# A two-layer diffusion block on one core: modulation vectors summed in 32-column groups of TensorE, and scan scores taken from 64-row halves

## The reference, cut to what matters

```python
def modulate(x, shift, scale):
    return rms(x) * (1.0 + scale) + shift

for layer in range(2):                                  # layer 0: scan mixers, layer 1: attention
    m_l = split(silu(c)     @ w_mod[layer] + b_mod[layer], 6)    # w_mod[layer]: 1024 x 6144
    m_c = split(silu(c_ctx) @ w_mod[layer] + b_mod[layer], 6)
    z = concat([modulate(xc, m_c[0], m_c[1]), modulate(xl, m_l[0], m_l[1])])
    if layer == 0:
        p = z @ even_w_in
        ya = rwkv7_mix(p[:A_PROJ])                      # a scan with a 64x64 state per head, 8 heads, 2 directions
        yb = rglru_mix(p[A_PROJ:])                      # a gated diagonal scan, 512 wide, 2 directions
        y = concat([ya, yb]) @ even_w_out
    else:
        y = diff_attention(z)
    x = x + m[2] * y
    x = x + m[5] * peer_ffn(modulate(x, m[3], m[4]))    # 8 heads x 16 experts per token, gathered from tables

def rwkv7_step(state, r, w, k, v, kk, akk):             # for each token, head and direction
    sa = state @ kk
    state = state * w - outer(sa, akk) + outer(v, k)
    return state, state @ r
```

## Time and profile before

| what | value |
|---|---|
| median of three runs | 3483.07 us (3481.43 to 3484.12) |
| the profiled execution | 3485.71 us, of which the span of the trace is 3483.9 us |
| busy share of the span | PE 80%, DVE 65%, POOL 31%, ACT 20% |
| `modulation` | 9.6 to 90.8 us |
| `project_even` | 111.6 to 333.8 us |
| `rglru` | 333.8 to 391.6 us |
| `rwkv_scan` | 391.6 to 957.5 us |
| the rest of layer 0 and all of layer 1 | 957.5 us to the end |
| DMA rate in the expert stages | 420 GB/s in most slices of the page |

### The profile page before, as it was taken

The page is one execution under the profiler, slowest core; times in us unless marked ns, Lnnn a source line. Parts: engine busy times, 40 slices in busy tenths (PEclk is TensorE's granted clock), DMA queues, the critical chain, the costliest instruction groups (busy, mean ns, idle before and its releaser), DMA issues. The chain is left out here.

```text
span 3483.9 us, 31043 instructions
## 1 busy us (share of the span) xinstructions
PE 2802.4 (80%) x8972; PEld 1425.2 (41%) x8972; DVE 2254.0 (65%) x5072; ACT 701.0 (20%) x1707; POOL 1090.5 (31%) x941
## 2 busy tenths in 40 slices
PE   7697399999967999777787878787696578887777
PEld 1242288888834444322232223232344344432222
DVE  7697423332343767788887888888244367787887
ACT  2112433233102111111111111111104111111111
POOL 0010232122011444444444444444000034444443
PEclk9798699899878999999999999999899899999999
DMA  8552000000014999999999999999300189999998
GB/s 315 185 195 90 33 1 1 1 1 1 1 73 180 362 378 371 413 420 420 420 413 420 421 420 413 418 420 410 148 24 3 74 347 420 420 415 420 421 420 342
DMA packets 133878, 927.54 MB, mean 266 GB/s; under 512 B 16764, under 2 KB 17788, under 8 KB 31380
## 3 DMA queue, kind: packets, MB, share of 16 engines
q0 software_dynamic: 113472, 830.62, 58.1%
q1 hardware_dynamic: 20312, 95.72, 7.4%
HBM read 925.13 MB, written 1.15 MB: 266 GB/s over the span
## 5 line engine op out<-in xcount | busy, mean ns | idle before, releaser
L1370 PE MATMUL psum<-ring,diag 128*128 128x512 f32 x3072 | 1483.8, 622 | 374.7 <-DVE diag L1459 372.7
L1267 POOL DMA_INDIRECT ring<-in_uv,experts x768 | 914.4, 1191 | 1375.4 <-PE psum L1370 1017.9
L1481 DVE CUSTOM_DVE_ANT_0 ring<-ring,hcur 128x1024 f32<-128x1024 f32 x768 | 941.5, 1226 | 261.0 <-DMA ring<-in_uv,experts 240.2
L1370 PEld LDWEIGHTS psum<-ring,diag 128*128 128x128 f32 x3072 | 557.4, 194 | 1276.5 <-DVE diag L1459 799.4
L1301 ACT ACTIVATE gel<-dots 128x1 f32<-128x1 f32 x768 | 143.6, 201 | 1325.4 <-DVE dots L1481 1324.8
L1459 DVE TENSOR_SCALAR diag<-ident,gel,wcur 128x128 f32<-128x128 f32 x768 | 256.8, 345 | 80.2 <-ACT gel L1301 78.0
L385 PE MATMUL psum<-zT,wring 128*128 128x512 f32 x368 | 164.3, 604 | 15.7 <-DMA wring<-in_w_in 15.7
L1015 DVE COPY_PREDICATED T<-level,psum 128x512 f32<-128x512 uint32 x80 | 58.7, 734 | 180.6 <-PE psum L820 180.6
L1350 PE MATMUL psum<-hT,w_q 128*128 128x512 f32 (+3 forms) x512 | 163.1, 473 | 1.4 <-DMA w_q<-in_w_q 1.4
L1543 PE MATMUL psum<-wring,zT 128*128 128x512 f32 x320 | 140.1, 601 | 10.2 <-DMA wring<-in_w_qkv 10.2
L444 DVE SCALAR_TENSOR_TENSOR acc<-wmod,scol,acc 128x512 f32<-128x512 f32 x168 | 126.3, 752 | 6.9 <-ACT acc L411 1.2
(11 more groups left out here) (314 smaller groups left out, 2903.9 us busy)
## 6 DMA issues: line engine op xcount, KB each, us to landing
wring<-in_w_mod SPq DMA_DIRECT2D x12, 2048.0 KB, 9.7
wmod<-in_w_mod POOLq DMA_DIRECT2D x12, 2048.0 KB, 8.4
w_q<-in_w_q SPq DMA_DIRECT2D x32, 512.0 KB
ring<-in_uv,experts POOLq DMA_INDIRECT x768
wring<-in_w_qkv SPq DMA_DIRECT2D x6, 2048.0 KB, 8.4
wring<-in_w_in SPq DMA_DIRECT2D x23, 512.0 KB, 5.0
bc<-modulation_rows SPq DMA_DIRECT2D x14, 512.0 KB, 5.5
w<-in_w_out SPq DMA_DIRECT2D x8, 512.0 KB, 6.2
```

Of the source, the lines that this page charges most:

```text
L1267: nc.gpsimd.indirect_dma_start(ring[:, s % RING], None, uv, bass.IndirectOffsetOnAxis(ap=experts[:, n, j:j + 1], axis=0)).then_inc(row_in[ ...
L1370: m = nc.tensor.matmul(ps[:, c], diag[:, j % DIAGS], ring[:, j % RING, D + 512 * c:D + 512 * c + 512], start=(first and j == 0), stop=(las ...
L1481: nc.vector.tensor_tensor_reduce(u, u, hcur[:], 1.0, 0.0, ALU.mult, ALU.add, dots[:, j:j + 1]).then_inc(dot_done, 1)
```

## The change

1. Modulation. All 8 row blocks go through PE. The stationary operand is now `scolz`, 32 columns wide, of which columns 2 to 31 are zero. Row block k writes the 32 PSUM partitions of group k mod 4, so four groups of 32 stationary columns are in use and each is written twice. ACT copies the bank out as it is, one more matmul with the selector `sel` adds the four groups (its column s is one on partitions 0+s, 32+s, 64+s, 96+s), and DVE adds the bias.
2. Layer 1's modulation moves from `project_even` into `rglru`. SP loads `w_mod[1]` there in half chunks of 1 MB (four row blocks) into four slots. The first four are issued at the end of `project_even`'s list. PE, ACT and DVE take the chunks between the units: two behind unit 1's gates, one behind each later unit's, the last four at the end.
3. Scores. `bF` and `kF` are kept per pair. A head's score matmul reads its own 64 rows of both operands, and ACT writes a pair's halves with one instruction. POOL's zeroing of the two tiles goes.
4. Outputs. For a pair of heads the four matmuls with 128 rows come first and then both with 64 rows. Their outputs stay 64 columns wide.

```diff
+def groups(nc, bank, scol, weight, ks):
+    for i, k in enumerate(ks):
+        g = 32 * (k % GROUPS)
+        m = nc.tensor.matmul(bank[g:g + 32], scol[:, k], weight[:, i], start=(k < GROUPS), stop=(k >= KD - GROUPS))
+    return m
...
 (modulation, PE)
-                    for k in range(SPLIT):
-                        m = nc.tensor.matmul(ps[0:2, n % BANKS], scol[:, k], wring[:, n % RING, k], start=(k == 0), stop=False)
+                    groups(nc, ps[:, n % 2], scolz, wring[:, n % RING], range(KD)).then_inc(part_mm, 1)
...
+                    nc.tensor.matmul(ps[0:2, 2 + n % 2], sel[:], acc[:, n % 2], start=True, stop=True).then_inc(sums_mm, 1)
...
 (project_even, SP; mod_sums, mod_row, add_sums and POOL's loads and stores are gone from this phase)
+                for i in range(MOD_RING):
+                    sp.dma_start(wmod[:, i], half_chunk(a, i)).then_inc(wmod_in[i], 16)
...
 (rglru)
+        MOD_AT = lambda u: range(u + (u > 0), u + 2 if u < 7 else MOD_CHUNKS)
+                for i in range(MOD_RING, 2 * MOD_CHUNKS):
+                    sp.wait_ge(part_mm, i - MOD_RING + 1)
+                    sp.dma_start(wmod[:, i % MOD_RING], half_chunk(a, i)).then_inc(wmod_in[i % MOD_RING], 16)
...
+                def mod_groups(n):
+                    if n >= 2:
+                        pe.wait_ge(acc_done, n - 1)
+                    for i in (2 * n, 2 * n + 1):
+                        pe.wait_ge(wmod_in[i % MOD_RING], 16 * (i // MOD_RING + 1))
+                        groups(...).then_inc(part_mm, 1)
+                    if n >= 1:
+                        add_groups(n - 1)
...
+                    if u >= 1:
+                        for n in MOD_AT(u - 1):
+                            mod_groups(n)          # PE; DVE has mod_row(n) at the same place of its loop
...
 (rwkv_scan)
-        bF = ph.sb("bF", [P, 2, HEADS, P])
+        bF = ph.sb("bF", [P, 2, PAIRS, P])
...
+                def scores(n, side, banks, ready, pair):
+                    for h in (2 * pair, 2 * pair + 1):
+                        i = 2 * (h // 4) + h % 2
+                        m = nc.tensor.matmul(ps[:, banks[i], place(h):place(h) + 256], side[half(h), n % 2, pair], qrF[half(h), n % 2, pair],
+                                             start=True, stop=True)
+                        if pair % 2:
+                            m.then_inc(ready, 1)
...
-                        for e in range(2):
-                            rows = slice(HD * e, HD * e + HD)
-                            nc.scalar.activation((bF, kF)[i - 2][rows, b, e:HEADS:2], ps[rows, 4 + i].rearrange("p (a t) -> p a t", a=PAIRS),
-                                                 ACT.Copy).then_inc(tr_done, 1)
+                        nc.scalar.activation((bF, kF)[i - 2][:, b], ps[:, 4 + i].rearrange("p (a t) -> p a t", a=PAIRS),
+                                             ACT.Copy).then_inc(tr_done, 1)
...
-                    for h in range(HEADS):
-                        o = ps[:, 1 + 2 * (h % 2), cols(h // 2)]
-                        nc.tensor.matmul(o, BF[:, h, 1], rkv[:, 2, t, cols(h)], start=True, stop=False)
-                        nc.tensor.matmul(o, NE[:, h, 1], U[:, cols(h)], start=False, stop=False)
-                        m = nc.tensor.matmul(o, RpF[half(h), h // 2], S0[half(h), h // 2], start=False, stop=True)
+                    for h0 in range(0, HEADS, 2):
+                        for h in (h0, h0 + 1):
+                            nc.tensor.matmul(o_of(h), BF[:, h, 1], rkv[:, 2, t, cols(h)], start=True, stop=False)
+                            nc.tensor.matmul(o_of(h), NE[:, h, 1], U[:, cols(h)], start=False, stop=False)
+                        for h in (h0, h0 + 1):
+                            m = nc.tensor.matmul(o_of(h), RpF[half(h), h // 2], S0[half(h), h // 2], start=False, stop=True)
```

More of the change, by code:

```diff
@@ L125, in constants, with modulation @@
     }
[L128 to L134 removed]
+def modulation(nc, a, mod, scol, sel):
+    RING = 3
     with Phase(nc) as ph:
@@ L774, in _ @@
                     scores_ae(n, 3)
-                    for i in range(4):
-                        if n >= 1 and i == 0:
-                            pe.wait_ge(s_done, n)
-                        if n >= 1 and i == 1:
-                            pe.wait_ge(r_done, n)
-                            pe.wait_ge(o_done, n)
-                        for h in heads_of(i):
-                            m = nc.tensor.matmul(ps[:, BF_BANKS[i], place(h):place(h) + 256], kF[:, b, h], qrF[:, b, h // 2],
-                                                 start=True, stop=True)
-                        m.then_inc(bf_mm, 1)
+                    if n >= 1:
+                        pe.wait_ge(s_done, n)
+                        pe.wait_ge(r_done, n)
+                        pe.wait_ge(o_done, n)
+                    for pair in range(4):
+                        scores(n, kF, BF_BANKS, bf_mm, pair)
                     for lv in range(LEVELS):
@@ L1776, in build @@
         scol = sb(ctx, "scol", [P, KD, 2])
-        ones = sb(ctx, "ones", [P, 2, 2])
-        modulation(nc, a, mod, scol, ones)
+        sel = sb(ctx, "sel", [P, 2])
+        modulation(nc, a, mod, scol, sel)
+        wmod_in = [nc.alloc_semaphore(f"wmod1_in{i}") for i in range(MOD_RING)]
         every, latents = list(range(TILES)), [2, 3]
```

242 lines of the change are left out of this document (99 added, 143 removed).

## The result

The changed kernel took 3405.6 us (median of four, 3395.51 to 3410.8) where the kernel before took 3482.25 (3481.06 to 3484.12): ratio 0.9776, 95% interval 0.9753 to 0.9799, 76.7 us less. The forecast was 3418, the range 3385 to 3490. The profiled execution took 3405.61 us, its span 3403.8, against 3485.7 and 3483.9 before. PE's busy time is 2727.3 us (still 80% of the span), DVE's share fell from 65% to 61%.

What follows compares the result with a forecast made beforehand. PE was taken to bound `rwkv_scan`, except one stretch of DVE masks, and DMA `modulation`, with PE busiest in `project_even`. Terms -6 - 47 + 32 - 19 - 6 - 19 = -65 from 3485.7 gave 3421, median 3418; range 3385 to 3490 us.

Steps and rivals of the forecast that it cites:

- Column groups overlap: Modulation chunks: instructions overlap only across a matmul's border, 9 slots, 3.8 us, plus 0.86 for the selector: 4.7 us.
- Rival 1's variant: Modulation's grouped matmuls run at the lower clock because of pauses for DMA; same sign as Rival 1, no separate chance.
- `modulation`, -6: First modulation stage: -3 us from chunks at 5.2 us, -3 from a shorter way from last landing to store.
- `project_even`, -47: Layer 1's modulation leaves this stage: earlier PE start -9, ten L377 groups gone -18, no tail -20 us.
- `rglru`, +32: Layer 1's modulation enters this stage: units of 6.4 us, scans queued behind row 7, end 423.4 instead of 391.6 us.
- My alternative for four-way overlap: In `rglru`, four-way overlap makes DMA's 5.0 us a unit the pace: +24 us.
- Scores, -19: Scan scores: overlapping row halves make DVE's masks the bound, -2.05 us in seven units, about -4.6 in unit 0.
- ACT, -6: Scan: two ACT copies of 64 partitions become one, -0.44 us twice a unit in seven units.
- Outputs, -19: Scan outputs: fewer row changes and overlapping 64-row matmuls cut a unit from 11.1 to about 8.7 us; ends -10 and -38.
- 2 and 3: Only column groups overlap, 3444 us, chance 0.14; only row halves overlap, 3483 us, chance 0.08, respectively.
- Rival 4: Scan scores: the lower clock lasts longer, +1.5 us a unit, +12 in all, 3430 us; chance included in the forecast's 0.54.
- 1: Neither column groups nor row halves overlap, so PE bounds both modulation places: +26, 3509 us; chance 0.16.

Runs made afterwards that it cites:

- e5: Changed kernel with neighbouring row blocks k and k+1 sharing a column group, same number of instructions; 3408.6 us (one run).
- e4: Changed kernel with all eight row blocks of a chunk written to one group of 32 partitions; 3491.8 us (one run).
- e2: Changed kernel with the old scan phase, so only the modulation's change remains; 3454.1 us, ratio 0.9923 to the kernel before.
- e3: Changed kernel with each head's three output matmuls in the old order (128, 128, 64 rows); 3431.2 us, ratio 0.9861 to the kernel before.
- e10: Changed kernel with the old scores, copies and zeroing, keeping the new output order and modulation; 3413.7 us, ratio 0.9800 to the kernel before.
- e6: Changed kernel with the kF scores in head order 0, 2, 1, 3, 4, 6, 5, 7; 3398.7 us (one run).
- e7: Changed kernel with the outputs' 128-row matmuls taking 128 moving columns instead of 64; 3398.8 us, ratio 0.9747 to the kernel before.

## Why the prediction was right, and which terms were off

The direction and the mechanisms held; the sum was 12 us short. One step, on how instructions of different groups follow each other, was wrong, and two terms of the scan were mis-sized because the clock was read as given.

- *Column groups overlap.* Held, and more than I counted: 1.74 us for 16 instructions, not 3.8. The step that failed is "a matmul's own two instructions still have the same group and follow each other, so only neighbours across a matmul's border overlap". They do follow each other, but the next group's go past them (e5). With four groups in use the price is a quarter, and DMA becomes the bound in both places. e4 shows the serial end at 6.98 us. Rival 1's variant, the groups at the lower clock, came true for five of `modulation`'s chunks (2.3 to 3.4 us each) and cost nothing behind the transfers.
- *`modulation`, -6.* Measured -8.3 at the store. First to last start are 55.1 us instead of 60.0: -5.0, where I said -3, with a pace of 4.9 us a chunk and not 5.2. From the last chunk's start to the store are 4.4 us instead of 8.8, where I said 6. The first chunk starts 1.0 us later, behind the transfer of `sel`, which I had left out.
- *`project_even`, -47.* Measured -49.5, from the three causes named: start after 4.3 us (-8.7), no L377 (-18), no tail behind the last projection (275.52, ACT's last copy's start, to the next phase at 276.88; -20.0). A further 2.7 us I had not counted: behind the shorter wait fewer projections ran at the lower clock (up to 132 us before, 6 us after PE's start; up to 114 after, 4 us).
- *`rglru`, +32.* Measured +26.2. The queue of row 7, scans and last rows is as described, 14.7 us of scans and a tail of 11.7 (349.2 to 360.9, I said 13); the pace is DMA's 5.0 us a unit and not PE's 6.4. My alternative for four-way overlap said +24.
- *Scores, -19, and ACT, -6.* With the old outputs that is what they give (24 us in the scan, e2 to e3); DVE's masks follow each other at 0.60 us and not at the 0.67 that I took. Behind the new outputs they give 9 to 11 (e10). The step that failed is to price the scores "half the price above, 0.43 us at the lower clock ..., and begin at the lower", and the outputs beside it as if each stood alone. Both draw on the same lower-clock time: 6.08 us from O to the first level behind outputs at the upper clock, 7.5 to 8.1 behind fallen ones (e10). How much of the 13 to 15 us between the two figures is that, and how much that e10 kept the clock in more units, the runs do not separate.
- *Outputs, -19.* Mis-sized: 42 alone, 28 to 29 behind the new scores. The working on the matmuls holds: a pair takes 1.37 us at the upper clock against 1.92 for two heads, 2.52 against 3.32 at the lower, and a unit whose clock fell took 8.6 us, where I said 8.7. What I put at the end of the range only, "the clock stays up through the stretch", happens in three or four of eight units (in one to four over all kernels with these outputs and scores). Over the scan, length times mean clock is 504 us before (565.9 x 0.89) and 472 after (512.7 x 0.92): about 32 us less at full speed, PE's waits included, and some 62 us lost to the lower level became some 41 (the clock's two digits leave 3 us open). I had given the clock no part.
- *Sum.* -44 for the scan was -53, the modulation's -21 was -30.7 by stages in the profile (-7.4 at the start of `project_even`, 111.60 to 104.21, -49.5, +26.2) and -26.8 by e2's median. Behind the scan the profile shows 3.8 us more in stages that nobody touched, within their spread of 6. Of my rivals, 1 is refuted by the 1.74 us and by e4, 2 and 3 by the rows of scores and groups. Rival 4 did not occur: the masks bind (5.56 us from O to the first level in most units), and where the clock had fallen it was up again 2.2 to 2.8 us after O (units 3 to 6), where in the kernel before it took 2.7 to 5.2.

The Trainium skill ("TensorE: Matmul & The Clock Gate", Part 3, measured speedups) gives up to about threefold for three or four groups; here four column groups gave 6.98 / 1.74 = 4.0. Its "What overlaps and what doesn't", taken strictly, would have given the serial end; the trace disagrees, since four column groups on the same 128 rows overlapped fully. Its PSUM Bottleneck ("TensorEngine Tiling (Array Packing)") is what happened in the scores: PE waits 0.30 and 1.30 us for DVE's masks.

## What to carry to other kernels

Matmuls with few stationary columns can be spread over the four column groups at a quarter of the time, in either order of issue that was tried here; whether that pays depends on DMA, which bound both places at once afterwards. Terms that touch one lower-clock stretch must not be added as if each were alone: read which level a stretch ran at, and price a neighbour at the level that it will find. Moving columns that cost next to no time (128 instead of 64) kept the clock up in 14 of 16 stretches here, and a clock that was kept up in one stretch fell in the next in two of them.

## What the runs showed of the hardware that I had not expected

- Four column groups on the same 128 rows run side by side: 16 instructions of 512 columns in 1.74 us, 6.98 in one group (e4).
- Instructions pass one another between groups: with neighbours in one group still 1.74 us, and a selector instruction started at 319.83 ahead of grouped ones at 320.24 and 320.67 that precede it in the program (e5). Two row halves do the same (e6, 2.07 us against 2.00).
- At the upper clock a float32 matmul with 128 moving columns follows the one before as closely as one with 64, at 0.22 us (two instructions). Only at the change from 64 rows back to 128 it cost a little more, so that DVE's wait for the outputs was 4.81 us (e7) against 4.60.
- The same program kept or lost the upper clock in different units in two executions (3 and 4 of 8 outputs), worth about 3.4 us each (7.95 - 4.60), and its times spread over 15 us (3395.5 to 3410.8) where the kernel before spread over 3 to 10; in its profile the clock was low in all eight outputs.
